# Moving work between stages in the second layer of a two-layer kernel: order of weight units, of the dt chain and of the turns

## The chip, the cores and the metric

The kernel runs on one core of one Trainium2 chip. The metric is the device time of one launch in microseconds (us): 1860.7 us is the median of three runs before the change (1860.04 to 1865.69).

Engines are named as the profile names them. PE is TensorE (matmuls and transposes; PEld its weight loads), DVE is VectorE, ACT is ScalarE, POOL is GpSimd, SP only issues the transfers of weights. Each engine runs its own list of instructions in order and waits on semaphores that the others raise.

## The reference, cut to what matters

The first block (an mLSTM and a sparse attention, then a mixture of 32 experts) is untouched by the change and is left out. The second block computes, for 256 tokens and a model width of 1024:

```python
h = rms_norm(x, norm_g) * (1 + scale) + shift
proj = h @ w_in
q, k, v, z_att, q_idx, k_idx, w_idx, z_ssm, xbc, dt_raw, gate_logits = split(proj)
q = partial_rope(rms_norm(q), ...); k = partial_rope(rms_norm(k), ...)
q_idx, k_idx = partial_rope(...), partial_rope(layer_norm(k_idx), ...)
o_att = sparse_attention(q, k, v, q_idx, k_idx, w_idx) * silu(z_att)      # top 64 causal keys
y_att = o_att @ w_branch_att
xs, bm, cm = split(silu(causal_conv(xbc) + conv_b))                         # 4 taps
dt = softplus(dt_raw + dt_bias); a = -exp(a_log)
y = ssd(xs, dt, a, bm, cm) + d_skip * xs                                    # chunks of 128
y = group_rms_norm(y * silu(z_ssm)) * ssm_norm_g
y_ssm = y @ w_branch_ssm
merged = sigmoid(g_att) * y_att + sigmoid(g_ssm) * y_ssm
x = x + gate * (merged @ w_out)
```

## The kernel before, in words

**Units of weights.** All of the second layer's weights pass through a list of 56 units (`UNITS2`) of 1 MB: 256 columns of a matrix with 1024 rows (or 128 columns of the one with 2048 rows). Units 0 to 7 give q, k, v, the indexer's parts and dt (unit 7 is only 100 columns wide); 8 to 11 (`U_ZA`) give z_att, the gate of the attention; 12 to 23 (`U_XBC`) feed the convolution; 24 to 39 (`U_ZS`) give z_ssm and the merging gates; 40 to 43 (`U_ATT`) are w_branch_att, 44 to 51 (`U_SSM`) w_branch_ssm, 52 to 55 (`U_OUT`) w_out. SP loads a unit into one of three raw slots (`load_unit`, L289) as soon as the unit three places earlier is done with its slot.

**Plain and split units.** A plain unit is multiplied in full fp32 straight from its slot, and the slot comes free when PE has used it. A split unit is first cut by ACT into a rounded high part (`make_high`, L1655) and by DVE into the rest (`make_low`, L1662), into one of three stages, and is multiplied in three cheaper passes (high with high, high with low, low with high); its slot comes free with the low part. Before, units 0, 1 and 12 to 23 are plain. `unit_by_tokens` (L1686) and `unit_by_columns` (L1698) are the two forms of the matmuls.

**Four programs, one after another.** The second layer is four `nc.Block()`s; at the end of each, every engine waits for all others.

1. Projections: PE runs units 0 to 7, DVE copies the results out of PSUM (L1770, L1773).
2. Attention (from L1822). PE calls `give(n)` for the next n of the 16 "halves", units 8 to 23, into the PSUM banks 0 and 1 in turn; ACT calls `take(n)` for them. A half of z_att is taken with one Silu into `azT` (L1861). A half of the convolution is taken with eight scaled copies (L1872, three of four into `taps`); POOL adds the taps (L1835) and ACT applies the Silu two halves later (`silu`, L1849). PE may give half h only when half h-2 is taken. Between the halves stand the steps of the attention: DVE normalises and rotates the index parts (L2004 to L2024), PE turns them (L1961, L1962), ACT and DVE form the norms of q and k (Square L1881, sums L2029, root L1885), DVE scales and rotates q and k (L2037 to L2040 and L1811 to L1816, twice), PE turns them (L1970), then logits (L1938), scores (L1946), the selection of keys on DVE (L2051 to L2072), exponentials on ACT (L1899), the turns of the probabilities (L1953, each copied by ACT, L1905) and the product with v (L1995, L1996).
3. State space (from L2127). PE turns xbc nine times (L2196) and ACT copies each (L2156, L2159); DVE works out dt and `adt` in 22 small steps (L2262 to L2279), PE sums them (L2201), DVE scales xs by dt (`y`, L2286). Then come eight pairs (chunk, group): `prepare(i)` on PE (L2213, L2216), masks and products on DVE (L2306, L2315), the exponential on ACT (L2165), the outputs (L2252), and between them two units each, called fills (units 24 to 39). Fills 16 to 19 are units 40 to 43 with the gated attention as the other factor, in its parts `inh` and `inl`.
4. Branch and output (from L2370). PE turns y (L2384), ACT and DVE form its parts yh and yl (L2417, L2441), PE multiplies by w_branch_ssm (L2394) and w_out, DVE adds the residual (L2461), PE turns the result, and it is stored.

The order in which the units stand in PE's program is written by hand; nothing plans it. Two lines set what is plain and what PE does between the turns of the probabilities:

```python
PLAIN = {0, 1} | set(range(U_XBC, U_ZS))
turn(1, 0); pe.wait_ge(sm("b_pt_ready"), 2); turn(1, 1); give(2)   # in short
```

Of the kernel before, what the change touches and what calls it, by code (L numbers as in the profile page):

```python
# [23 lines left out]
P = 128  # L24
# [129 lines left out]
UNITS2 += [("w_in_2", 0, [(0, P_QI, 256)]), ("w_in_2", 0, [(0, P_QI + 256, 68), (68, P_DT, 32)])]  # L154
U_ZA = len(UNITS2)
UNITS2 += halves("w_in_2", 0, P_ZA) + halves("w_in_2", 0, P_ZA + 512)
U_XBC = len(UNITS2)
UNITS2 += sum((halves("w_in_2", 0, P_XBC + 512 * n) for n in range(6)), [])
U_ZS = len(UNITS2)
# [9 lines left out]
PLAIN = {0, 1} | set(range(U_XBC, U_ZS))  # L169
# [32 lines left out]
def two_layers(nc, A, cst_in, c32_in, out):  # L202
    with ExitStack() as ctx:
# [1501 lines left out]
        bc = sb("bc", [P, 2 * HD + 2 * ID + 3 * SH])  # L1705
        att2 = ctx.enter_context(ExitStack())
# [71 lines left out]
        with ExitStack() as pi:  # L1778
# [12 lines left out]
            tmp = sb("tmp", [P, SEQ], at=pi)  # L1791
# [9 lines left out]

            HALVES = U_ZS - U_ZA
            ZHALVES = U_XBC - U_ZA
# [18 lines left out]
            with nc.Block() as block:  # L1822
# [6 lines left out]
                def _(pool):  # L1829
                    G.done(pool, pool.memset(taps[:], 0.0), sm("taps_zero"))  # L1830
                    for i in range(HALVES - ZHALVES):
                        pool.wait_ge(sm("half_taken"), ZHALVES + i + 1)
# [9 lines left out]
                def _(act):  # L1842
# [9 lines left out]
                    def take(count):  # L1852

                        for _ in range(count):
                            h = taken[0]
                            if h >= 2 and U_ZA + h + 2 in SPLIT:
                                make_high(act, U_ZA + h + 2)
                            act.wait_ge(sm("u_used"), U_ZA + h + 1)
                            src = ps[:, h % 2, :].rearrange("p (j t) -> p j t", j=2)
                            if h < ZHALVES:  # L1860
                                S.done(act, act.activation(azT[:, 2 * h:2 * h + 2, :], src, ACT.Silu), sm("half_taken"))  # L1861
                            else:
                                i = h - ZHALVES
# [13 lines left out]
                    make_high(act, U_ZA + 2)  # L1877
                    act.wait_ge(sm("var_ready"), 1)
                    S.done(act, act.activation(var[:], var[:], ACT.Sqrt), sm("dev_ready"))
                    for t in range(TT):  # L1880
                        S.done(act, act.activation(sq2[:], qkv[:, t, 0:NH * HD], ACT.Square), sm("head_sq"))  # L1881
                        if t == 0:
                            make_high(act, U_ZA + 3)
                        act.wait_ge(sm("head_sums"), t + 1)
                    S.done(act, act.activation(ssum[:], ssum[:], ACT.Sqrt), sm("head_rms"))  # L1885
# [4 lines left out]
                    take(3)  # L1890
# [27 lines left out]
                    for i in range(HALVES - ZHALVES - 2, HALVES - ZHALVES):  # L1918
                        silu(i)
# [176 lines left out]
        with ExitStack() as pj:  # L2096
# [31 lines left out]
            with nc.Block() as block:  # L2128
# [59 lines left out]
                def _(pe):  # L2188
# [66 lines left out]
                    for f in range(16, 20):  # L2255
                        fill(f)
# [246 lines left out]
```

## Time and profile before the change

| What | Value |
|---|---|
| median of three runs | 1860.7 us |
| the profiled execution | 1861.18 us |
| its span, first to last instruction | 1859.4 us |
| second layer in that span | from about 1379 us to the end |
| PE busy | 1740.1 us, 94% of the span |
| DVE busy | 555.9 us, 30% |
| ACT busy | 415.5 us, 22% |
| POOL busy | 106.4 us, 6% |
| mean granted clock of PE, in parts of full speed | 0.972 |

Times of rows are us from the start of the span. The profiled execution lies 0.5 us above the median, and 1.8 us of it lie outside its span. A matmul's end is modelled, so the pace of PE is read from starts: two groups of eight matmuls that start 0.96 us apart cost 0.12 us a matmul, whatever duration stands beside each. One fp32 matmul is two records.

### The profile page before, as it was taken

How to read it: one execution, taken by the hardware profiler on the slowest of the kernel's cores; microseconds unless marked ns; L12 is line 12 of the kernel's file. 1: busy time of each engine (PE TensorE's matmuls, PEld its weight loads, DVE VectorE, ACT ScalarE, POOL GpSimd, SP SyncE). 2: the span in 40 equal slices, each digit the busy share in tenths (PEclk: the TensorE clock that was granted, in tenths of full speed). 3: DMA queues.
4: the chain of work that ended last, by engine and by line, in shares of the span. 5: the costliest groups of instructions: out<-in, count | busy, mean ns of one | idle time of the engine just before them, and what ended most of it. 6: DMA issues, size and time to landing. Idle time of an engine off the chain costs nothing. (4 is left out here: it accounts for less than half of the span.)

```text
span 1859.4 us, 39736 instructions
## 1 busy us (share of the span) xinstructions
PE 1740.1 (94%) x17331; PEld 1017.3 (55%) x17331; DVE 555.9 (30%) x770; ACT 415.5 (22%) x692; POOL 106.4 (6%) x121
## 2 busy tenths in 40 slices
PE   6999998999999999999999999999859798799888
PEld 4875652343434434343443434344449787698888
DVE  2273172121111112111111211111346551676754
ACT  2344152000000000000000000000034266355442
POOL 0111020000000000000000000000000044110000
PEclk9999989999999999999999999999979899899999
DMA  9987395999999999999999999999616243333452
GB/s 344 345 286 244 133 338 210 388 396 407 401 397 399 399 398 395 400 398 393 392 403 404 394 399 397 399 398 408 226 51 196 63 135 93 113 116 112 136 148 80
DMA packets 187878, 545.45 MB, mean 293 GB/s; under 512 B 16216, under 2 KB 90216, under 8 KB 154952
## 3 DMA queue, kind: packets, MB, share of 16 engines
q1 hardware_dynamic: 172432, 519.49, 74.0%
q10 hardware_dynamic: 10968, 15.40, 2.3%
q0 software_dynamic: 4416, 9.69, 1.6%
q8 instruction: 44, 0.72, 0.2%
q14 instruction: 18, 0.15, 0.0%
HBM read 526.06 MB, written 17.84 MB: 293 GB/s over the span
## 5 line engine op out<-in xcount | busy, mean ns | idle before, releaser
L1428 PE MATMUL ps<-ring_low,xg 128*32 128x512 f32 x3072 | 344.6, 597 | 0.0
L1428 PE MATMUL ps<-first_ring,xg 128*32 128x512 f32 x3072 | 335.4, 592 | 0.0
L1559 DVE TENSOR_SCALAR gl<-ps 128x768 f32<-128x768 f32 x32 | 30.6, 957 | 684.1 <-PE ps L1428 684.1
L1428 PEld LDWEIGHTS ps<-first_ring,xg 128*32 128x32 f32 x3072 | 99.5, 110 | 230.1 <-issue 230.1
L1428 PEld LDWEIGHTS ps<-ring_low,xg 128*32 128x32 f32 x3072 | 96.4, 110 | 206.6 <-issue 200.8
L1451 PE MATMUL ps<-first_ring,aT 128*32 128x256 f32 x3072 | 173.3, 382 | 2.3 <-ACT aT L1510 2.3
L1451 PE MATMUL ps<-raw_more,aT 128*32 128x256 f32 x3072 | 171.6, 379 | 0.0
L1451 PEld LDWEIGHTS ps<-first_ring,aT 128*32 128x32 f32 x3072 | 100.4, 111 | 82.5 <-issue 20.2
L1504 ACT ACTIVATE sg<-gl 128x768 f32<-128x768 f32 x32 | 27.0, 844 | 510.8 <-DVE gl L1559 510.8
L1451 PEld LDWEIGHTS ps<-raw_more,aT 128*32 128x32 f32 x3072 | 99.9, 110 | 65.9
L1662 DVE TENSOR_TENSOR low<-ring_low,high 128x2048 fp32r<-128x2048 f32 x42 | 98.7, 2350 | 121.5 <-ACT high L1655 121.0
L1509 ACT ACTIVATE aT<-ps 128x576 f32<-128x576 f32 x32 | 20.8, 650 | 445.5 <-PE ps L1439 435.7
L1655 ACT ACTIVATE high<-ring_low 128x2048 fp32r<-128x2048 f32 x42 | 80.4, 1915 | 65.8 <-PE ps L2394 20.5
L1570 DVE COPY ye<-ps 128x768 f32<-128x768 f32 x32 | 30.6, 957 | 212.1 <-PE ps L1451 212.1
L1698 PE MATMUL ps<-hT,ring_low 128*128 128x256 f32 x384 | 86.1, 386 | 0.0
L1698 PEld LDWEIGHTS ps<-hT,ring_low 128*128 128x128 f32 x384 | 74.5, 195 | 10.6 <-ACT xbc L1872 0.3
L1398 POOL DMA_INDIRECT got<-y_dram,dest x8 | 7.6, 952 | 1075.8 <-DMA y_dram<-ye 1074.6
L1698 PE MATMUL ps<-inh,high 128*128 128x256 f32 x320 | 49.0, 293 | 16.1 <-ACT azT L1861 7.8
L321 PE MATMUL ps<-hT,first_ring 128*128 128x256 f32 x256 | 58.7, 389 | 1.8 <-ACT hT L514 1.8
L321 PEld LDWEIGHTS ps<-hT,first_ring 128*128 128x128 f32 x256 | 49.2, 194 | 11.5 <-issue 4.7
L1698 PEld LDWEIGHTS ps<-inh,high 128*128 128x128 f32 x320 | 43.2, 198 | 17.1 <-ACT azT L1861 8.1
L1835 POOL TENSOR_TENSOR xbc<-xbc,taps 128x512 f32<-128x512 f32 x36 | 46.1, 1279 | 102.5 <-ACT xbc L1872 100.5
(487 smaller groups left out, 1879.6 us busy)
## 6 DMA issues: line engine op xcount, KB each, us to landing
first_ring<-in_w_up_dram SPq DMA_DIRECT2D x128, 1024.0 KB, 6.6
ring_low<-in_w_up_dram SPq DMA_DIRECT2D x128, 1024.0 KB, 6.3
raw_more<-in_w_down_dram SPq DMA_DIRECT2D x64, 1024.0 KB, 6.7
first_ring<-in_w_down_dram SPq DMA_DIRECT2D x64, 1024.0 KB, 6.7
ring_low<-in_w_in_dram SPq DMA_DIRECT2D x39, 1024.0 KB, 5.3
first_ring<-in_w_ada_dram SPq DMA_DIRECT2D x7, 2048.0 KB, 20.3
ring_low<-in_w_ada_dram SPq DMA_DIRECT2D x5, 2048.0 KB, 18.2
y_dram<-ye ACTq DMA_DIRECT2D x32, 288.0 KB, 5.7
```

Of the source, the lines that this page charges most:

```text
L321: mm = pe.matmul(ps[:, bank, (j % 2) * SEQ:(j % 2 + 1) * SEQ], slots[n % len(slots)][:, k, j * P:(j + 1) * P], src[:, k, :], start=(k == 0 ...
L1398: pool.indirect_dma_start(got[:, t, BUFFER[j], :], None, y_dram[0:TOTAL, :], bass.IndirectOffsetOnAxis(dest[:, t, j:j + 1], 0))\
L1428: mm = pe.matmul(ps[32 * q:32 * q + 32, u, :], xg[:, k, 32 * block_of:32 * block_of + 32], w[:, :, 256 * f:256 * f + 256], start=False, st ...
L1451: mm = pe.matmul(ps[32 * q:32 * q + 32, 5 + u, 0:256], aT[:, f, 32 * block_of:32 * block_of + 32], w[:, 256 * part:256 * part + 256], star ...
L1504: act.activation(sg[:], gl[:], ACT.Sigmoid, scale=ALPHA).then_inc(s(tag, "sig_ready"), 1)
L1509: act.activation(aT[:, 0:6, :], flat[:, :, 0:ROWS], ACT.Copy).then_inc(s(tag, "aT_ready"), 1)
L1559: dve.tensor_scalar(gl[:], ps[:, 0:3, 0:256], LIMIT, None, ALU.min).then_inc(s(tag, "glu_ready"), 1)
L1570: dve.tensor_copy(ye[:], ps[:, 5:8, 0:256]).then_inc(s(tag, "ye_copied"), 1)
L1655: act.activation(high[:, s_ % STAGES], raw2[u % RAWS], ACT.Copy).then_inc(sm("u_high"), 1)
L1662: dve.tensor_tensor(low[:, s_ % STAGES], raw2[u % RAWS], high[:, s_ % STAGES].bitcast(F32), ALU.subtract)\
L1698: mm = pe.matmul(ps[:, bank, j * SEQ:(j + 1) * SEQ], a[:, k, j * P:(j + 1) * P], x[:, k, :], start=(i == 0), stop=(i == len(todo) - 1))
L1835: ins = pool.tensor_tensor(c, c, taps[:, i % 2, tap], ALU.add)
```

## The change

Nothing is computed that was not computed before; what moves is this.

- Units: the second half of z_att (two units) goes behind the convolution's twelve, so the halves are now z_att 0 and 1 (h = 0, 1), convolution 0 to 11 (h = 2 to 13), z_att 2 and 3 (h = 14, 15). Unit 7 and the first two of w_branch_att become plain.
- Attention: ACT takes two halves ahead of the second Square; PE gives two halves, and then one, around the turn of q and k, and one half between the turns (1, 0) and (1, 1). POOL clears only the first three columns of `taps`. The dt chain runs on DVE behind the probabilities, with its two exponentials on ACT in front of `exps(0)`; it lies in `rt`, the rotation's buffer, and `tmp` in `kd`.
- State space: the product of the attention with its gate opens DVE's program of this block. The sums of adt come first on PE, the nine turns use three banks and are copied by ACT and DVE two to one, fill 0 stands ahead of `prepare(0)`, and xs is scaled by dt one pair at a time. Fills 16 and 17 are plain; `inl` is formed after the last pair.
- Branch and output: fills 18 and 19 move into this block, behind the fourth and the eighth turn of y. w_out's units work in two banks each, and the residual is added after every second unit.

The diff, cut to its core:

```diff
-UNITS2 += halves("w_in_2", 0, P_ZA) + halves("w_in_2", 0, P_ZA + 512)
+UNITS2 += halves("w_in_2", 0, P_ZA)
 U_XBC = len(UNITS2)
 UNITS2 += sum((halves("w_in_2", 0, P_XBC + 512 * n) for n in range(6)), [])
+UNITS2 += halves("w_in_2", 0, P_ZA + 512)
...
-PLAIN = {0, 1} | set(range(U_XBC, U_ZS))
+PLAIN = {0, 1, U_ZA - 1} | set(range(U_XBC, U_ZS - 2)) | {U_ATT, U_ATT + 1}
...
-            tmp = sb("tmp", [P, SEQ], at=pi)
+            tmp = kd[:].rearrange("p t d -> p (t d)")
...
-                    G.done(pool, pool.memset(taps[:], 0.0), sm("taps_zero"))
+                    G.done(pool, pool.memset(taps[:].rearrange("p a b c t -> p (a b c) t")[:, :, 0:3], 0.0), sm("taps_zero"))
...
-                    make_high(act, U_ZA + 2)
                     act.wait_ge(sm("var_ready"), 1)
                     S.done(act, act.activation(var[:], var[:], ACT.Sqrt), sm("dev_ready"))
-                    for t in range(TT):
-                        S.done(act, act.activation(sq2[:], qkv[:, t, 0:NH * HD], ACT.Square), sm("head_sq"))
-                        if t == 0:
-                            make_high(act, U_ZA + 3)
-                        act.wait_ge(sm("head_sums"), t + 1)
-                    S.done(act, act.activation(ssum[:], ssum[:], ACT.Sqrt), sm("head_rms"))
+                    S.done(act, act.activation(sq2[:], qkv[:, 0, 0:NH * HD], ACT.Square), sm("head_sq"))
                     take(2)
                     act.wait_ge(sm("i_turned"), 1)
...
-                    take(3)
+                    act.wait_ge(sm("head_sums"), 1)
+                    S.done(act, act.activation(sq2[:], qkv[:, 1, 0:NH * HD], ACT.Square), sm("head_sq"))
+                    act.wait_ge(sm("head_sums"), 2)
+                    S.done(act, act.activation(ssum[:], ssum[:], ACT.Sqrt), sm("head_rms"))
+                    take(2)
                     act.wait_ge(sm("q_turned"), 1)
...
-                    take(3)
+                    take(4)
+                    S.done(act, act.activation(aexp, bcv("a_log_2"), ACT.Exp), sm("a_exp"))
+                    act.wait_ge(sm("dt_abs"), 1)
+                    S.done(act, act.activation(u_, u_, ACT.Exp), sm("dt_exp"))
                     exps(0)
...
                     mm.then_inc(sm("i_turned"), 1)
-                    give(3)
+                    give(2)
                     pe.wait_ge(sm("i_ready"), 1)
                     pe.wait_ge(sm("q_rotated"), TT)
...
                     mm.then_inc(sm("q_turned"), 1)
+                    give(1)
                     pe.wait_ge(sm("q_ready"), 1)
...
                     turn(1, 0)
+                    give(1)
                     pe.wait_ge(sm("b_pt_ready"), 2)
                     turn(1, 1)
-                    give(2)
+                    give(1)
...
-                    make_low(dve, U_ZA + 2)
...
-                    make_low(dve, U_ZA + 3)
...
+                    dve.wait_ge(sm("dt_exp"), 1)
+                    V.link(dve, dve.tensor_scalar(z_, u_, 2.0, None, ALU.add))
...
-                    for u in range(U_ZS, U_ZS + 2):
+                    for u in range(U_ZS - 2, U_ZS + 2):
                         make_low(dve, u)
-                    dve.wait_ge(sm("b_att"), 1)
-                    dve.wait_ge(sm("half_taken"), ZHALVES)
-                    V.link(dve, dve.tensor_tensor(azT ...
...
+            TURNS = [(0, 2), (1, 2), (0, 4), (0, 0), (1, 0), (0, 1), (1, 1), (0, 3), (1, 3)]
+            TURNED_IN = (0, 6, 7)
...
-                    pool.wait_ge(sm("adt_ready"), 1)
-                    pool.wait_ge(sm("xs_ready"), 9)
+                    pool.wait_ge(sm("xs_turned"), 2)
...
-                    pe.wait_ge(sm("xs_ready"), 9)
+                    pe.wait_ge(sm("az_gated"), 1)
+                    fill(0)
+                    pe.wait_ge(sm("xs_ready"), 6)
+                    pe.wait_ge(sm("xs_copied"), 3)
+                    pe.wait_ge(sm("cum_copied"), 1)
                     prepare(0)
...
-                    for f in range(16, 20):
+                    for f in range(16, 18):
                         fill(f)
...
+                    V.done(dve, dve.tensor_tensor(azT ..., ps[:, 2:6, :] ..., ALU.mult), sm("az_gated"))
...
-                    for t in range(TT):
-                        ins = dve.tensor_tensor(yv, xs[:, t, :] ..., dts[:, t, :] ..., ALU.mult)
...
                     for i, (c, g) in enumerate(PAIRS):
+                        V.link(dve, dve.tensor_tensor(heads(y[:, c, gw]), heads(xs[:, c, gw]),
+                                                      dts[:, c, gh].unsqueeze(2).to_broadcast([P, GH, SP]), ALU.mult))
...
-                    make_low(dve, U_ATT + 2)
+                    dve.wait_ge(sm("in_high"), 2)
+                    V.done(dve, dve.tensor_tensor(inl[:], azT[:], inh[:].bitcast(F32), ALU.subtract), sm("in_low"))
...
+                    for u in range(U_ATT + 2, U_SSM):
+                        make_low(dve, u)
...
+                    turn(range(4))
+                    unit_by_columns(pe, U_ATT + 2, 4, None, (inh, inl))
+                    turn(range(4, 8))
+                    unit_by_columns(pe, U_ATT + 3, 5, None, (inh, inl))
                     pe.wait_ge(sm("yh_ready"), 16)
...
-                        dve.wait_ge(sm("u_used"), U_OUT + k // 2 + 1)
+                        dve.wait_ge(sm("u_used"), U_OUT + 2 * (k // 4) + 2)
```

## Rows read from the trace of the kernel before

**Rows 1.** The page, busy time of an engine, its share and its instructions.
```profile
PE 1740.1 (94%) x17331; PEld 1017.3 (55%) x17331; DVE 555.9 (30%) x770; ACT 415.5 (22%) x692; POOL 106.4 (6%) x121
```

**Rows 2.** PE's waits from 1380 us on: us in total, times, longest.
```profile
PE ps L1698 <- ACT azT L1861: 7.8, 1, 7.8
PE ps L2213 <- DVE y L2286: 6.7, 1, 6.7
PE ps L1953 <- ACT qT L1905: 4.6, 1, 4.6
PE ps L2196 <- PEq L1822: 4.4, 1, 4.4
PE ps L2394 <- issue: 3.5, 1, 3.5
PE ps L1938 <- ACT kT L1894: 3.5, 1, 3.5
...
PE ps L1698 <- issue: 3.4, 1, 3.4
PE ps L2252 <- DVE xbc L2315: 2.7, 2, 2.5
PE ps L2213 <- DVE xbc L2306: 2.2, 6, 0.5
```

**Rows 3.** Timeline of PE: start, us, instructions, idle before them.
```profile
1424.54 1.00 PE L1686 MATMUL ps<-high,inh 128*128 128x100 f32 x8
...
1431.63 1.23 PE L1698 MATMUL ps<-inh,high 128*128 128x256 f32 x8 [1.63 <-PEq L1715]
...
1438.94 1.12 PE L1698 MATMUL ps<-inh,high 128*128 128x256 f32 x8
...
1444.70 0.38 PE L1961 MATMUL ps<-cst,idt 128*128 128x128 f32 x2
...
1466.36 7.07 PE L1698 MATMUL ps<-hT,ring_low 128*128 128x256 f32 x32
...
1610.30 1.95 PE L2216 MATMUL ps<-cst,xbc 128*128 128x128 f32 x16
```

**Rows 4.** A stretch in windows: engines' busy us, then granted clock, DMA share, GB/s.
```profile
1430.00:1436.10 6.10, 4.47 (x26) 4.50 (x26) 5.17 (x12) 3.20 (x2) 2.66 (x1) 0.72 0.56 169
```

**Rows 5.** Timeline of DVE and of ACT in the attention's first 50 us.
```profile
1451.51 0.28 DVE L2034 RECIPROCAL ssum<-ssum 128x20 f32<-128x20 f32 x1 [0.41 <-ACT ssum L1885]
...
1462.26 0.32 DVE L1816 TENSOR_TENSOR qkv<-rt 128x160 f32<-128x160 f32 x1
...
1473.52 1.20 ACT L1872 ACTIVATE taps<-ps,cols 128x253 f32<-128x253 f32 x3 [6.30 <-PE ps L1698]
```

**Rows 6.** Timeline of DVE and of POOL where both work in SBUF.
```profile
1508.83 1.37 DVE L2059 TENSOR_TENSOR sc<-sc,cst 128x256 f32<-128x256 f32 x1
...
1518.77 0.42 DVE L2065 TENSOR_TENSOR sc<-sc,cst 128x256 f32<-128x256 f32 x1
...
1508.38 1.54 POOL L1835 TENSOR_TENSOR xbc<-xbc,taps 128x512 f32<-128x512 f32 x1 [2.96 <-ACT xbc L1872]
```

**Rows 7.** Timeline of DVE: a step of dt, one of the loop, the residual.
```profile
1586.00 0.20 DVE L2265 TENSOR_SCALAR z_<-u_ 128x64 f32<-128x64 f32 x1 [1.40 <-ACT u_ L2150]
...
1655.60 0.69 DVE L2330 TENSOR_TENSOR t<-xs,bc 128x512 f32<-128x512 f32 x1
...
1853.14 1.00 DVE L2461 SCALAR_TENSOR_TENSOR xT<-ps,mod,xT 128x256 f32<-128x256 f32 x2 [4.75 <-PE ps L1698]
```

**Rows 8.** Timeline of ACT where y is turned.
```profile
1771.11 8.07 ACT L2417 ACTIVATE yh<-ps,cols 128x256 fp32r<-128x256 f32 x16 [5.72 <-PE ps L2384]
```

**Rows 9.** The page, transfers: issuer, count, KB each, median us to landing.
```profile
ring_low<-in_w_in_dram SPq DMA_DIRECT2D x39, 1024.0 KB, 5.3
```

**Rows 10.** Timeline of DVE: a low part that meets POOL, and one that does not.
```profile
1612.68 3.88 DVE L1662 TENSOR_TENSOR low<-ring_low,high 128x2048 fp32r<-128x2048 f32 x1
...
1631.00 2.29 DVE L1662 TENSOR_TENSOR low<-ring_low,high 128x2048 fp32r<-128x2048 f32 x1 [4.48 <-ACT high L1655]
```

## What the change will do to the time

> **What bounds the kernel now.** I read the page first. PE is busy for 94% of the span [rows 1], so its idle time is nearly all that a new order can win. Then PE's waits in the second layer [rows 2]: one long stall per stage. The six largest rows are 7.8, 6.7, 4.6, 4.4, 3.5 and 3.5 us, then come 3.4 and 2.7. Then PE's timeline [rows 3], for what a unit costs: the split unit from 1438.94 to 1444.70 costs 5.76 us, a plain one 32 records of 7.07 us, less a tail 6.9 us, and the 100 wide unit 7 takes from 1424.54 to the 1.63 us of idle before 1431.63, 5.5 us. A stall costs more than itself. The unit that starts at 1431.63 takes until 1438.94, 7.3 us against 5.76, and the window around it shows a granted clock of 0.72 of full [rows 4]: after the pause PE works for a while at the lower of its two levels (1.2 instead of 2.4 GHz). I price that at 1.5 us a stall [rows 3], up to 2.5 where turns follow.
>
> **The start of the attention.** Unit 7 plain: no row shows 100 columns in fp32. The nearest are fp32 records of 128 columns, 16 of them in 1.7 us by starts (the row says 1.95 with its tail) [rows 3], so 32 cost 3.4 us; by the plain unit's price it would be 6.9 at most, by columns alone 2.7. At 3.4 PE is done 2.0 us sooner, but the block ends with DVE's copy of idt, which stands behind the low part of unit 9. I take 0.9 us: **+0.9**.
>
> The 7.8 us before azT go. ACT was stuck between the two Squares and could not take the first half; now it takes it when PE has made it, at about 1439.9, and PE gives convolution 0 and 1 right behind the turn of the index parts (from about 1444.6 to 1458.4, two times 6.9). With the cold clock that is +9.3. The 3.5 us before the logits go too, covered by the third half, with their cold clock +4.9.
>
> But something is late next: q and k. Before, the scaling and rotation ran from 1451.51 to 1462.58 [rows 5], 11.1 us, and ended long before PE came. Now PE comes at 1458.4. ACT's second Square waits for the index turn (1444.6), the sums and the root come behind it, so DVE starts at about 1450.5, and alone would end at 1461.5. It is not alone. **DVE and POOL block each other**: an addition of 256 elements takes 0.42 us when POOL rests, and 1.37 us when it was asked at 1508.83, 0.45 us into an addition of POOL's, which ended at 1509.92 [rows 6]; it simply ran behind it. POOL's took 1.54 there. So where DVE works from SBUF to SBUF without a pause, each of POOL's additions (about 1.27 us) comes on top. ACT's copies of a half take about 3 us (three of eight in 1.20 [rows 5]), so convolution 0 reaches POOL at 1454.6 and convolution 1 at 1461.5: three additions each, 6 x 1.27 = 7.6 us, both inside DVE's stretch. q is ready at about 1469, and PE stands from 1458.4 for 10.4 us and then 2.0 more by the clock: -12.4. The bounds are 2.8 us of wait (no blocking, then 1.2 of clock) and 12 us (a table load of ACT more). I take the blocking because the rotation is of the same kind as the row's addition, two operands in SBUF. Together **+1.8**.
>
> The GPSIMD Engine Reference of the Trainium skill (section Specifications) says that GpSimd shares these with VectorE and contends with DVE instructions that have two SBUF inputs or a two-port mode. It speaks against this change, since it covers the rotation's small steps, which no row shows next to POOL; without it the wait would be 2.8 us. The row in [rows 6] agrees for an addition.
>
> **The rest of the attention.** The 4.6 us before turn (1, 1) are filled by a split unit of 5.76 us; with the cold stretch behind them (turns and the next unit, 2.5): **+7.0**. Its parts have to be there: the transfer can start when convolution 9 is used and lands 5.3 us later [rows 9], ACT and DVE need 4.2 more, and PE comes 15 us later. The block ended with ACT waiting for POOL's last addition and two Silus, 4.4 us of PE [rows 2]; now two units of z_att lie behind the convolution, and only the change of block stays, about 0.6: **+3.8**. dt's 22 steps of 0.20 us and more [rows 7] move into DVE's pause behind the probabilities. They too can meet six additions of POOL; that cover is about 10 us wide, and if it is gone, units 22 to 25 are late.
>
> **The start of the state space.** PE stood 6.7 us for `y` and, before that, ran nine turns at ACT's pace in the cold. From the block's start to fill 0 were 19.3 us, 3.8 of them `prepare(0)`. Now nothing waits for dt: the sums (0.8) and nine turns (4.7) with a short wait for DVE's copies, then fill 0, at about 6.7 us. Of the 15.5 before, 8.8 are saved, and 1.5 by the clock in `prepare(0)`; 0.7 to 0.8 come back, since no fill stands any longer between `prepare(0)` and `prepare(1)`, which waits for DVE's mask: **+9.5**.
>
> **The loop.** PE waits 6 times for DVE's mask, up to 0.5 us [rows 2]: the loop's circle runs through DVE and ACT, and PE follows. The change puts one more product into that circle in each pair, by the row of the same shape 0.69 us with 0.03 between [rows 7], six times in front of a `prepare`: **-4.4**. At its end the 2.5 us before the last outputs go, since units 40 and 41 are plain and ACT and DVE have no parts to make: **+2.5**.
>
> **Units 40 to 43 and the turn of y.** Before, from the last output to the first unit of w_branch_ssm, 41.2 us: 3.4 wait and 1.7 clock, four units 23.0, 2.4 between, and 10.1 for the turns, at ACT's pace of 1.0 us each [rows 8], 3.5 of it a plain wait. Now two plain units (13.8, 2.3 dearer than split) run beside DVE's last norm. Unit 43 can be fetched only when 40 is used, lands 5.3 us later [rows 9], is cut by ACT and DVE (4.2), and two products follow: the block ends 18.6 us behind the last output, PE having stood for 4.8. Then turns 2.1, a unit 5.8, turns 2.1, a unit 5.8, and 2.0 by the clock: 36.4. ACT and DVE are done with yh and yl before that. **+4.7**.
>
> **The end.** w_branch_ssm starts warm (1.6) and the second wait inside w_out's first unit goes (0.8): **+2.4**. But four residuals of 0.5 us [rows 7] follow the last matmul instead of two: **-1.0**.
>
> **The sum**: 0.9 + 1.8 + 7.0 + 3.8 + 9.5 - 4.4 + 2.5 + 4.7 + 2.4 - 1.0 = 27.2 us. From the profiled execution's 1861.2 that is 1834.0; it lies 0.5 above the median, so 1833.5 us, 1.5% less.
>
> **The rivals.**
> - POOL does not hold up the rotation: the wait for q is 2.8 us. For it: most of DVE's steps in the trace run alone, and the small ones may slip in between. Against: [rows 6]. It gives 8.4 more, 1825.
> - A collision inside the loop: the low part takes 3.88 us where it meets POOL and 2.29 where it does not [rows 10], and it begins only just behind POOL's work. If the new product shifts them onto each other in seven pairs, 7 x 1.6 = 11 us: 1845. Against: both start from the same event, so they should shift together.
> - The gaps only move: every stall returns behind the next step, and the time is 1860. Against: PE's work is the same and the new waits that I find have other work in front.
> - Slower: DVE as a whole becomes the bound in the attention. POOL's 36 additions of 1.27 us are 46 us; if DVE waits for all of them, 38 more than in my sum, at the rotation, the key selection and dt's chain, PE stands for each and the time is 1872. It decides once more than 27 us of them fall on a path that PE waits for; most fall on steps with slack, and before one met DVE for 1 us.
>
> **Chances.** The forecast's own mechanism 0.50, no blocking 0.25, the loop's collision 0.13, gaps that only move 0.04, slower 0.03; 0.05 for others, on the faster side. A run of this kernel can tell 0.3%, 5.6 us, from no change. So faster 0.93, same 0.04, slower 0.03. The range reaches from 1821 (no blocking, and the clock's costs halved) to 1846 (the collision).
>
> **What would show it.** In PE's waits: no azT, kT or qT row; a new row of L1970 behind DVE's rotation, some 10 us long, with DVE's L1811 to L2040 stretched while POOL adds; L2286 gone; `prepare` behind L2306 with about 1.2 us each; a gap of some 5 us before the turn of y. If the rotation's steps keep their 0.32 and 1.49 us while POOL works, the blocking step is wrong. If PE's wait for L2306 stays at half a microsecond, the loop is not bound by DVE. The forecast is wrong if the total of PE's waits falls by less than 15 us.

## The result and the profile after the change

The changed kernel takes **1830.25 us** (median of four runs, 1829.04 to 1831.8). Beside it the kernel before took 1863.14 us (four runs, 1860.04 to 1865.69). The ratio is 0.982, with a 95% interval from 0.9808 to 0.9833. A second series of the changed kernel (e11) gave 1830.61 (1829.72 to 1831.48), ratio 0.983 (0.9813 to 0.9846). The forecast was 1833.5, 27.2 us less than before; by the medians it is 32.9 us less. Part of that difference is the starting point: the median before the change that the forecast started from, 1860.7, lies 2.4 us below the one of all four runs.

The profiled execution took 1831.8 us with a span of 1830.0 and a mean granted clock of 0.978. The page's busy times, which answer to [rows 1]:

```profile
PE 1727.2 (94%) x17283; PEld 1004.4 (55%) x17283; DVE 562.6 (31%) x777; ACT 410.7 (22%) x688; POOL 106.8 (6%) x121
```

PE's waits from 1380 us on, against [rows 2] (us in total, times, longest):

```profile
PE ps L1688 <- PEq L220: 9.7, 1, 9.7
PE ps L1980 <- DVE qkv L1823: 9.3, 1, 9.3
PE ps L2386 <- PEq L2155: 6.5, 1, 6.5
PE ps L2230 <- DVE xbc L2310: 5.3, 7, 1.1
PE ps L2258 <- DVE xd L2301: 2.8, 3, 0.9
PE ps L2417 <- DVE inl L2489: 1.6, 1, 1.6
PE ps L1700 <- PEq L1719: 1.6, 1, 1.6
PE ps L2220 <- DVE bt L2289: 1.3, 1, 1.3
PE ps L2209 <- PEq L1829: 0.3, 1, 0.3
```

The first row is the entry into the second layer. It is ahead of that layer's first unit in both kernels, and is not counted below. The rest is 28.7 us, against 48.1 in the same view of before: 19.4 less. azT, kT, qT and `y` are gone. Three waits carry what is left: L1980 (the turn of q, behind the rotation), L2386 (the turn of y, behind the end of a block) and the loop's two rows, L2230 and L2258. PE's busy time fell as well, by 12.9 us, though its work is nearly the same. 11.3 us of it fell in the second layer, where the granted clock is 0.97 on average instead of 0.95: fewer stalls are followed by the slow clock.

By starts of PE's instructions, the stages add up as follows (before, after, gain in us). They sum to the 29.4 us between the two spans. That is less than the 32.9 us between the medians, since the profiled execution of the kernel before is a short one of its kind (1861.18 us) and that of the changed kernel the longest of its four.

| Stage | before | after | gain | forecast |
|---|---|---|---|---|
| everything ahead of the second layer | 1378.95 | 1380.10 | -1.15 | 0 |
| units 0 to 6 | 45.59 | 45.33 | +0.26 | 0 |
| unit 7 and the change of block | 7.09 | 5.34 | +1.75 | +0.9 |
| unit 8 to the turn of the index parts | 13.07 | 11.58 | +1.49 | 0 |
| from there to the end of the attention | 139.42 | 124.87 | +14.55 | +12.6 |
| start of the state space to the first outputs | 34.58 | 24.99 | +9.59 | +9.5 |
| the loop, first to eighth outputs | 118.84 | 120.32 | -1.48 | -1.9 |
| eighth outputs to the first unit of w_branch_ssm | 43.00 | 39.92 | +3.08 | +4.7 |
| w_branch_ssm and w_out | 72.33 | 69.95 | +2.38 | +2.4 |
| last turns and the end | 6.53 | 7.60 | -1.07 | -1.0 |
| sum | | | +29.4 | +27.2 |

The first line is work that the change does not touch. It moves from profile to profile: the second layer starts between 1377.16 and 1384.10 us in the profiles of this study. So two experiments are compared by their second layers too, from the first unit's start to the start of the last turns: 473.92 us before, 442.30 after.

### The profile page after: what moved, and what is told of

The parts are those of the page before. It is cut to its first block and busy times, and to the rows that moved or that the text cites. A ratio compares the mean times of both kernels' runs of the same rounds, so it can differ in the third digit from the quotient of the medians.

```text
span 1830.0 us, 39634 instructions
## 1 busy us (share of the span) xinstructions
PE 1727.2 (94%) x17283; PEld 1004.4 (55%) x17283; DVE 562.6 (31%) x777; ACT 410.7 (22%) x688; POOL 106.8 (6%) x121
## 5 line engine op out<-in xcount | busy, mean ns | idle before, releaser
L1664 DVE TENSOR_TENSOR low<-ring_low,high 128x2048 fp32r<-128x2048 f32 x39 | 91.4, 2346 | 73.4 <-ACT high L1657 73.0
L1657 ACT ACTIVATE high<-ring_low 128x2048 fp32r<-128x2048 f32 x39 | 74.7, 1916 | 43.1 <-PE ps L2404 17.3
L348 POOL DMA_DIRECT2D mrows<-mrow x56 | 28.1, 509 | 187.7 <-ACT mrow L341 187.7
L1424 PE MATMUL ps<-bup,one 96*32 96x512 bf16 x384 | 27.3, 386 | 8.2 <-ACT xg L1502 8.2
```

The source lines that it names most:

```text
L348: eng.dma_start(mrows[at:at + 4, :], mrow[32 * q:32 * q + 1, i % 2, :].rearrange("a (j p) -> a j p", p=P))\
L1424: pe.matmul(ps[32 * q:32 * q + 32, u, :], one3[:], cols_of, start=True, stop=False)
L1657: act.activation(high[:, s_ % STAGES], raw2[u % RAWS], ACT.Copy).then_inc(sm("u_high"), 1)
L1664: dve.tensor_tensor(low[:, s_ % STAGES], raw2[u % RAWS], high[:, s_ % STAGES].bitcast(F32), ALU.subtract)\
```

## The experiments

Diffs are against the changed kernel unless they say otherwise. "The layer" is the second layer's length as just defined.

**1. POOL held back until q and k are rotated** (e1). POOL's first sum of taps waits for the rotation; its three sums of the convolution's first half are then late, but nothing needs them yet.

```diff
                         pool.wait_ge(sm("half_taken"), XBC0 + i + 1)
+                        if i == 0:
+                            pool.wait_ge(sm("q_rotated"), TT)
```

> The changed kernel, but POOL's first convolution additions wait until q and k are rotated. Theory (POOL's six additions of 1.27 us block DVE's steps): the rotation's steps keep 0.33, 0.42, 1.2 and 1.5 us, DVE's stretch from its first step (L2044) to the last shrinks from 17.0 to 11.1 us by 6 us or a little less, PE's wait for q falls from 9.3 to about 3.3 us, with a little less of the slow clock behind it, and the time from 1830.3 to about 1823.5 us. Rival (the wait is long because DVE starts late, behind ACT's second Square and the root): the wait stays at 8 to 9 us and the time within 1.5 us of 1830.

Measured: 1823.05 us (1822.36 to 1824.5), ratio to the kernel before 0.9786 (0.9768 to 0.9804), and 7.6 below the changed kernel's second series. The layer is 435.76. First the changed kernel's DVE and then its POOL, by their timelines (start, us, instructions, idle before):

```profile
1452.98 0.33 DVE L1819 TENSOR_TENSOR rt<-qkv,sin 128x160 f32<-128x160 f32 x1
1453.34 1.44 DVE L1820 TENSOR_TENSOR rt<-qkv,cos 128x160 f32<-128x160 f32 x1
1454.82 1.31 DVE L1821 TENSOR_TENSOR rt<-qkv,sin 128x160 f32<-128x160 f32 x1
1456.16 1.31 DVE L1822 TENSOR_TENSOR qkv<-rt 128x160 f32<-128x160 f32 x1
...
1460.65 1.37 DVE L2050 TENSOR_TENSOR qkv<-qkv,bc 128x256 f32<-128x256 f32 x1
1462.05 1.27 DVE L1818 TENSOR_TENSOR rt<-qkv,cos 128x160 f32<-128x160 f32 x1
1463.36 1.30 DVE L1819 TENSOR_TENSOR rt<-qkv,sin 128x160 f32<-128x160 f32 x1
1464.69 0.33 DVE L1820 TENSOR_TENSOR rt<-qkv,cos 128x160 f32<-128x160 f32 x1
...
1453.34 3.96 POOL L1842 TENSOR_TENSOR xbc<-xbc,taps 128x512 f32<-128x512 f32 x3 [22.63 <-ACT xbc L1882]
1460.25 4.23 POOL L1842 TENSOR_TENSOR xbc<-xbc,taps 128x512 f32<-128x512 f32 x3 [2.96 <-ACT xbc L1882]
```

The same engines in e1, and its wait:

```profile
1450.91 0.33 DVE L1820 TENSOR_TENSOR rt<-qkv,cos 128x160 f32<-128x160 f32 x1
...
1457.89 8.00 POOL L1844 TENSOR_TENSOR xbc<-xbc,taps 128x512 f32<-128x512 f32 x6 [29.63 <-DVE qkv L1823]
1474.28 3.96 POOL L1844 TENSOR_TENSOR xbc<-xbc,taps 128x512 f32<-128x512 f32 x3 [8.38 <-ACT xbc L1884]
...
PE ps L1982 <- DVE qkv L1823: 3.3, 1, 3.3
```

Six DVE steps, one for each addition of POOL's, take 1.27 to 1.44 us instead of 0.33 or 0.42. That adds 5.9 us; in e1 all keep their length, and the wait falls from 9.3 to 3.3. The expectation's rival, that DVE starts late, falls: DVE's first step comes 69.0 us after the layer's start in both.

**2. The loop's product moved into its slack** (e2, e10). In e2 the scaling of xs for pair i+1 stands behind `seg_ready` of pair i. In e10 both chunks are scaled at once, ahead of the loop.

```diff
-V.link(dve, dve.tensor_tensor(y of pair i, xs, dts, ALU.mult))   # in front of the mask of pair i
+if i == 0: scale(0)
...
                                                       ALU.min), sm("seg_ready"))
+if i + 1 < len(PAIRS): scale(i + 1)
```

> The changed kernel, but the scaling of xs by dt for the next pair stands right behind the mask of this pair, where DVE waits for ACT, instead of in front of the next mask. Theory (the loop's circle runs through DVE and ACT, and the product lengthens it by 0.72 us a pair): PE's waits for L2310 and L2301 fall from 8.1 us together to about 3 to 4, and the time by 4 to 5 us, to about 1825.8. Rival (PE bounds the loop, the waits are only its reading): no change beyond 1 us.

> The changed kernel, but xs is scaled by dt at once in front of the loop, two products of 2.3 us as before the change, with fill 0 where the change put it. Theory (the product lengthens the loop's circle, and at the start of the stage DVE has slack behind fill 0: it is idle from 1577.5 to 1581.8 but for that one product): 4.4 us less than the changed kernel, as with the scaling in the slack, and nothing lost in front: about 1825.8. Rival (the bulk products come back onto the path in front of the first mask): 2 us or more are lost again, 1828 and above.

Measured: e2 1825.47 us (1824.99 to 1825.9), ratio 0.9798 (0.978 to 0.9815), layer 437.47; e10 1824.72 (1823.58 to 1825.46), ratio 0.9798 (0.9781 to 0.9814). The loop of e2 takes 115.95 us instead of 120.32. PE's waits in e2, against 5.3 and 2.8 above, and the same to the digit in e10:

```profile
PE ps L2230 <- DVE xbc L2317: 3.1, 7, 0.8
PE ps L2258 <- DVE xd L2308: 0.6, 3, 0.2
```

The waits give 4.4 us and the loop 4.4. So the product was on the circle that PE follows: where it stood it cost most of its 0.72 us a pair, and where e2 or e10 put it, about nothing.

**3. The block's end** (e3, e12). In e3 the two gated products of units 40 and 41, the low part of unit 43, and SP's load of unit 46 move into the next block; e12 moves SP's load alone.

```diff
-                    for u in range(U_ZS + 2, U_SSM + 3):      # SP in the state space's block
+                    for u in range(U_ZS + 2, U_SSM + 2):
...
-                    for u in range(U_SSM + 3, len(UNITS2)):   # SP in the last block
+                    for u in range(U_SSM + 2, len(UNITS2)):
```

> The changed kernel, but unit 43's low part and the two gatings of fills 16 and 17 stand at the start of DVE's next program instead of at the end of this one. Theory one (as read in the trace of after: DVE works without a pause from the last output to the end of the block, so DVE sets its end): PE's wait of 6.5 us in front of the turn of y falls by about 3.5 us, the slow stretch behind it by up to 1 us, the time to about 1826 us. Theory two (as forecast: the transfer of unit 43, which waits for the plain unit 40, and its high part set the end): the block ends only when ACT has the high part of unit 43, 1728.4 in the trace of after, and the wait falls too but ends there: a difference of at most 3.7 us, and the last instruction before the block's end is ACT's. Rival: the work pushed behind the turns delays yl and w_branch_ssm by what was gained: 1830.

> The changed kernel with SP's load of unit 46 moved behind the boundary of the last block, and nothing else; the low part of unit 43 and the two gated products stay ahead of it. In the changed kernel DVE was through at 1732.11, but the next block's first turn started at 1734.76, and SP's load of unit 46, which waits for that low part, takes 1730.82 to 1734.31. Theory: the last of the three ends the block, so with SP's load gone the block ends with DVE, the turns start 0.5 to 1.2 us behind its last product (0.53 in the row of the kernel before), from the seventh output to the first turn it is 20.3 to 20.9 us instead of 22.2, and the time falls by 1.5 to 2, to about 1828.7. Rival 1: DVE alone held the block and the 2.6 us behind it are the change of blocks itself; then the stretch stays at 22.2 and the time at 1830.4. Rival 2: the load is late at the other end, unit 46 comes too late for PE and a wait of over 1 us appears in the units of w_branch_ssm, so that the time stays or rises.

Measured: e3 1823.21 us (1822.9 to 1826.79), ratio 0.9791 (0.9771 to 0.9811), layer 436.45; e12 1828.7 (1826.7 to 1830.78, five runs), ratio 0.982 (0.9806 to 0.9833). The changed kernel's DVE, SP and PE around the boundary (timeline):

```profile
1726.30 4.49 DVE L1664 TENSOR_TENSOR low<-ring_low,high 128x2048 fp32r<-128x2048 f32 x2
1730.71 1.40 DVE L2354 TENSOR_TENSOR ring_low<-ring_low,ps 128x512 f32<-128x512 f32 x2
...
1730.82 3.49 SPq L291 DMA_DIRECT2D ring_low<-in_w_branch_ssm_dram  x1
...
1734.76 3.65 PE L2386 MATMUL ps<-cst,y 128*128 128x128 f32 x16 [6.47 <-PEq L2155]
```

e12's:

```profile
1728.39 4.50 DVE L1664 TENSOR_TENSOR low<-ring_low,high 128x2048 fp32r<-128x2048 f32 x2
1732.81 1.40 DVE L2354 TENSOR_TENSOR ring_low<-ring_low,ps 128x512 f32<-128x512 f32 x2
...
1734.76 3.36 PE L2386 MATMUL ps<-cst,y 128*128 128x128 f32 x16 [4.37 <-PEq L2155]
```

and e3's SP and PE:

```profile
1725.94 1.78 SPq L291 DMA_DIRECT2D ring_low<-in_w_branch_ssm_dram  x1
...
1728.17 1.94 PE L2379 MATMUL ps<-cst,y 128*128 128x128 f32 x16 [2.67 <-PEq L2155]
```

In the changed kernel DVE is done at 1732.11 and SP's issue at 1734.31; the turns start 0.45 us behind SP. In e3 it is 0.45 behind SP again (1725.94 + 1.78 = 1727.72), DVE having ended at 1725.79. In e12 DVE is done at 1734.21 and the turns start 0.55 behind it. So the last of them ends the block, and SP counts.

What makes SP late is not DVE's low part alone. The issue of unit 46 starts 0.03 us behind that low part, and then lasts 3.49 us. It is the third load in 2.5 us: unit 44's was issued at 1728.32, when PE was done with unit 41, and unit 45's at 1728.73. Unit 44 landed 6.1 us after its issue, at 1734.44, by this row of the transfers (the last figure is the time from issue to landing):

```profile
ring_low<-in_w_branch_ssm_dram SPq DMA_DIRECT2D x1, 1024.0 KB, 6.1
```

The issue of unit 46 ended at 1734.31, 0.13 us before that. In all eight profiles that have these three loads (the changed kernel's, e1, e2, e4, e6, e10, e11 and e12) that issue ended within 0.16 us of unit 44's landing, also in e12, where it started at 1734.71 and lasted 1.75 us. So in the changed kernel the block's end follows the landing of unit 44; whether a faster DVE alone would have brought it forward was not tried, and these rows speak against it. What the issue waits for is not shown beyond this coincidence.

From the eighth outputs to the turns it is 22.23 us, 20.14 in e12 and 18.44 in e3. The late load of e12 costs nothing: its waits have no row for it. Its layer is 437.28 us, 5.0 shorter than the changed kernel's, but only 3.1 of that lie around the boundary; 1.3 come from units 0 to 6 and 0.6 from the attention, which the edit does not touch. Its median is 1.9 below the second series of the changed kernel (e11), with ranges that overlap, so the conclusion rests on the rows.

**4. Fill 0 back behind the first `prepare`** (e4).

```diff
-                    fill(0)
                     pe.wait_ge(sm("xs_ready"), 6)
...
-                        if i:
-                            fill(2 * i)
+                        fill(2 * i)
```

> The changed kernel, but fill 0 stands behind the first prepare again. Theory (the 9.6 us of this stage come from dt's chain and the bulk scaling having left the path, not from fill 0's place): PE waits 1 to 2 us more for the copies in front of prepare, and the 0.85 us wait for the first mask goes: 0 to +1.5 us, 1830.3 to 1831.8. Rival (fill 0 covers the stage's waits): +4 us or more, 1834 and above.

Measured: 1831.93 us (1831.52 to 1832.54), ratio 0.9831 (0.9814 to 0.9849). From the state space's start to the first outputs 25.07 us, against 24.99. Its median is 1.3 us above the second series of the changed kernel, but the second layer is as long (442.53 us against 442.30). What the place of fill 0 wins in front it loses as the wait of `prepare(1)`. So the 9.6 us owe nothing to it. By the waits 6.7 of them are dt's chain (the row of `y` in [rows 2]); how the rest divides between the turns' copies and the clock was not tried apart.

**5. Single parts put into the kernel before** (e5, e8). e5 gives one half between turn (1, 0) and turn (1, 1), e8 makes unit 7 plain; diffs against the kernel before.

```diff
                     turn(1, 0)
+                    give(1)
                     pe.wait_ge(sm("b_pt_ready"), 2)
                     turn(1, 1)
-                    give(2)
+                    give(1)
```

```diff
-PLAIN = {0, 1} | set(range(U_XBC, U_ZS))
+PLAIN = {0, 1, U_ZA - 1} | set(range(U_XBC, U_ZS))
```

> The kernel before, with one line of the change alone: the last half but one is given between turn (1, 0) and turn (1, 1). Theory (a stall costs itself and the slow clock behind it, 4.6 + 2.5 us): the wait of L1953 goes and the time falls by 7.0 us. Rival (the gap moves to the end of the block, where ACT and POOL finish the last half): the wait at the block's end, 4.4 us, grows by what was gained, and the time stays within 1.5 us.

> The kernel before, with unit 7 plain alone. Theory (read from the trace of after: unit 7 costs PE 1.75 us less, and the stretch behind it is not at the slow clock, 1.5 us, but the wait for azT is set by ACT and DVE, which start only 1.75 us sooner): unit 8 takes 5.8 us instead of 7.3, the wait for azT grows from 7.8 to about 9.3, and the time falls by 1.8 us. As forecast (DVE's low part of unit 9 holds the block's end): 0.9 us. Rival: all of it stays, 3.3 us.

Measured: e5 1859.24 us (twelve runs, 1857.62 to 1862.27), ratio 0.9977 (0.9968 to 0.9986), so 0.23% or 4.3 us gained. By the stages the turns' part is 7.4 shorter, and the next two are 1.9 and 1.3 longer. PE's wait at the end of that block in e5, against 4.4 in [rows 2]:

```profile
PE ps L2197 <- PEq L1822: 6.3, 1, 6.3
```

The 1.9 us come back there, since ACT and POOL end the block at their own pace (in e5 POOL adds six times without a pause, from 1569.96 to 1579.89, and ACT's last Silu ends at 1580.89), and PE only arrives sooner. With the z_att units behind the convolution this wait is 0.3 us, so there the half between the turns keeps its price. These stages add up to 4.2 us, as the medians have it. The profiled execution's whole layer, though, is as long as before (473.84 us against 473.92): the other 4.1 us went in stages that the edit does not touch, ahead of the turns of the probabilities and in w_branch_ssm. e8 took 1861.79 (twelve runs, 1859.81 to 1865.61), ratio 0.999 (0.9981 to 0.9999). It starts unit 8 1.75 us sooner, as the changed kernel does, and unit 8 runs 1.5 faster; by the start of the first plain unit all but 0.6 is given back: the wait for azT is 8.4 instead of 7.8, and the turn of the index parts waits 1.6 us for DVE. (Its profiled execution is its longest, 1865.61 us, so its layer, 476.77, says nothing of the gain.) DVE was held by POOL's clearing of `taps`, by e8's timeline:

```profile
1431.45 2.23 DVE L2006 TENSOR_SCALAR idt<-idt,mean 128x64 f32<-128x64 f32 x1
...
1430.97 2.66 POOL L1830 MEMSET taps<- 128x3072 f32 x1 [78.64 <-POOLq L1715]
```

The same step takes 0.26 us a moment later. In the kernel before it was held for the same 2.23 us, but PE came later. The change clears three columns only (0.13 us of POOL), an edit that I had named and not costed, and takes two low parts of 2.29 us out of the same stretch of DVE. The 2.0 us of the clearing alone cover the 1.6; the two edits were not tried apart.

**6. The third half ahead of q's turn** (e6).

```diff
-                    give(2)      # behind the turn of the index parts
+                    give(3)
...
-                    give(1)      # behind q's turn
```

> The changed kernel, but PE gives the third half in front of the turn of q and k instead of behind it. Theory (DVE sets when q is ready, at 1466.2, whatever PE does): the wait for q falls by 6.9 us to 2.4, but ACT's copies of q and k, 3.5 us, are uncovered behind it; together 3.4 us less wait and up to 1 us less at the slow clock: 1826 to 1827. Rival (a third half keeps ACT and POOL busy earlier and holds DVE up again): no gain, 1830.

Measured: 1827.08 us (1825.99 to 1829.2), ratio 0.9811 (0.9795 to 0.9828), 3.5 less than the changed kernel's second series. PE's waits in e6:

```profile
PE ps L1948 <- ACT kT L1902: 3.0, 1, 3.0
...
PE ps L1980 <- DVE qkv L1823: 2.4, 1, 2.4
```

The 9.3 us become 2.4, and kT's wait comes back, 3.0 us where [rows 2] had 3.5. A unit can cover one of the two; holding POOL back (e1) is worth twice as much.

**7. All three together, and the tail** (e7, e9). e7 is e1, e2 and e3 in one. e9 also gives w_out's last two units one bank each, so that only two residuals follow the last matmul.

> The changed kernel with the three edits together that each took some us: POOL's first additions behind the rotation, the scaling in DVE's slack, unit 43's low part behind the block's end. If they act in different stages they add up: 1830.3 - 7.2 - 4.8 - 7.0 = 1811.3 us. If one only exposes another's wait, 1815 or more.

> The same three, and w_out's last two units in one bank each as before the change, so that two residuals instead of four follow the last matmul: 1.0 us less than with the three alone, about 1810.3 us. If the tail is set by something else (the copies, the store), no change against it.

> The changed kernel once more, unchanged, as the mark for the two runs beside it, because the first layer, which no edit touches, has begun the second up to 3 us sooner or later from kernel to kernel: 1829 to 1832 us, with the second layer's stages as in the first profile within 1.5 us together.

Measured: e7 1816.12 us (1814.89 to 1816.56), ratio 0.9742 (0.9723 to 0.976), layer 426.89; **e9 1815.15** (1813.17 to 1815.7), ratio 0.9736 (0.9717 to 0.9755), layer 426.73, which beats both kernels, the changed one by 15 us. The three parts shorten the layer by 6.5, 4.8 and 5.9 us alone, 17.2 in all, and by 15.4 together. PE's waits in e7:

```profile
PE ps L1982 <- DVE qkv L1823: 3.3, 1, 3.3
PE ps L2232 <- DVE xbc L2319: 3.1, 7, 0.8
PE ps L2390 <- PEq L2157: 2.8, 1, 2.8
```

They are those of the single runs. What is missing is clock. The turns of y and the two units among them take 16.68 us in e7 and 15.03 in e3, which is 1.65 of the 1.8 us, though PE stood for 2.8 and 2.7 us ahead of them. The four us around the first turns in windows, e3 and then e7 (busy time of PE, PEld, DVE, ACT and POOL, then granted clock, DMA share, GB/s):

```profile
1728.00:1732.00 4.00, 3.83 (x34) 3.86 (x35) 3.76 (x4) 2.97 (x7) 0.00 (x0) 1.00 1.16 308
```

```profile
1720.60:1724.60 4.00, 4.00 (x23) 4.00 (x23) 3.90 (x5) 2.91 (x7) 0.00 (x0) 0.60 1.18 303
```

e11 is the changed kernel again, as above. e9's tail is not told from e7 by the medians, whose ranges overlap. The profiles show it: from the last turns to the end it is 6.55 us in e9 and 7.58 in e7 (7.56 to 7.68 in all ten profiles with the change's w_out), the 1.0 us that was expected.

## Why the prediction was right, and where its steps were off

The direction, the mechanism of each large term and the size were right: 27.2 us forecast for the profiled execution, 29.4 measured. That the sum came so near is in part luck. Three stages gave 4.3 us more than forecast (unit 7, unit 8, the rest of the attention), the units 40 to 43 gave 1.6 less, and the first layer, which nobody touched, took 1.15 back in this profile.

**The start of the attention.** The price of unit 7 held: 3.71 us, where the forecast had 3.4 and the kernel before 5.46 (7.09 less the 1.63 of idle). PE's timeline:

```profile
1425.43 3.71 PE L1688 MATMUL ps<-ring_low,hT 128*128 128x100 f32 x32
1430.77 1.19 PE L1700 MATMUL ps<-inh,high 128*128 128x256 f32 x8 [1.63 <-PEq L1719]
```

I had taken only 0.9 of the 2.0 us, since DVE's copy stands behind the low part of unit 9. But unit 7 takes no stage any longer, so unit 9's parts wait for unit 5 and not for unit 6. They are done early, DVE's copy waits for PE alone (4.94 us idle ahead of it), and 1.75 came, the whole price of unit 7. And unit 8 now runs at the full clock (below), 1.5 us that I had not counted.

**q and k, and the blocking.** The step forecast a wait of 10.4 us, and 9.3 came, ending at 1466.2 where about 1469 was forecast. Experiment 1 shows the mechanism, and with it the first rival (1825, no blocking) falls. DVE began at 1449.1, 1.4 us earlier than I had it. And POOL cost 5.9 us, not 7.6: I had put 1.27 on top for each addition, but a stretched step is 1.31 in all, so it costs 1.31 - 0.33 = 0.98; DVE's own 0.33 lies beside an addition of POOL's, and the pace of the first three, 1.32 (3.96 in all), is the one that they have with DVE idle. The Trainium skill has this in SBUF — State Buffer (section Terms): the port pair that VectorE and GpSimd share is locked for a whole instruction, and the other engine blocks. The trace agrees for the 160 element steps, 0.33 us alone and about 1.3 next to POOL.

The fear for dt's chain came true as well: six of its steps met POOL. One of them in the changed kernel's DVE timeline, behind a step that did not:

```profile
1534.23 0.23 DVE L2099 TENSOR_TENSOR rt<-rt 128x64 f32<-128x64 f32 x1
1534.48 1.27 DVE L2100 TENSOR_SCALAR rt<-rt 128x64 f32<-128x64 f32 x1
```

No wait of PE's answers to them; the pause behind the probabilities held.

**The clock behind the stalls** was rightly counted. The changed kernel in windows (columns as in experiment 7): unit 8; PE's wait and then the turn of q; the wait before and the turn of y.

```profile
1430.00:1436.00 6.00, 5.24 (x44) 5.27 (x45) 4.64 (x23) 2.77 (x3) 0.13 (x1) 1.00 0.99 313
...
1457.00:1466.20 9.20, 0.00 (x0) 0.00 (x0) 8.82 (x12) 3.02 (x8) 4.37 (x4) 0.69 0.38 114
1466.20:1470.50 4.30, 4.26 (x20) 4.29 (x21) 0.38 (x2) 0.00 (x0) 0.00 (x0) 0.50 0.02 4
...
1728.00:1734.70 6.70, 0.29 (x2) 0.00 (x0) 4.07 (x4) 0.35 (x1) 0.00 (x0) 0.92 0.84 224
1734.70:1738.00 3.30, 3.24 (x16) 3.27 (x17) 0.99 (x3) 1.99 (x5) 0.00 (x0) 0.50 1.19 292
```

0.50 is the lower of the two levels, 1.2 GHz of 2.4. The 20 transposes of q and k take 4.3 us there and the first 16 of y 3.3, against 1.7 for 16 in the full clock (1.67 from start to start, 1744.94 to 1746.61). I had added 2.0 us in each place; it was 2.2 behind the wait for q, and at the turn of y 1.6 and 1.1 more in the unit behind it (6.88 against 5.76).

**The rest of the attention** gained 14.6 us with the above, against 12.6 forecast. The block's end gave 4.1 (3.8). The rest, 10.5, is the turns' part and the stage of q, forecast 8.8; how much falls to each depends on what is allowed for plain and split units that changed places between them. **The start of the state space** was 9.6 (9.5).

**The loop.** The step "the change puts one more product into that circle" was right in kind and in size: experiment 2 takes the product out of the circle and gains 4.4 us, the term of the sum. PE's single waits in the loop are 0.5 to 1.1 us, where about 1.2 each was forecast. The loss of the stage was 1.5 us, where 1.9 was forecast. The second rival (1845) needed the low parts to collide with POOL in seven pairs; in the changed kernel one low part is stretched, to 3.36 us in the first pair, as one was before, and all later ones take 2.29.

**Units 40 to 43 and the turn of y** is the term that was mis-sized most, 3.1 instead of 4.7, by its step "the block ends 18.6 us behind the last output, PE having stood for 4.8". PE stood for 6.5. The clock took 0.7 more than I had, and the turns without it 0.8 less (1.7 for 2.1, twice), so the wait is what was mis-sized. The step took the transfer of unit 43 as what is late. The rows of experiment 3 show otherwise: unit 43 landed at 1726.40 and its high part was done at 1728.35, before DVE was through with the low part of unit 42. DVE works without a pause into the boundary, and behind it SP's last load ends the block, 2.2 us later. I had counted the products but not SP, which every block waits for too, nor that the issue of its third load in a row would last until the first had landed. (The waits and stretches that I listed for this stage before the change add up to 40.6 us and not to 41.2; by starts it is 43.0 less the 1.7 of the outputs, 41.3.)

**The end** came as worked out. The total of PE's waits fell by 19.4 us, above the 15 below which I had called the forecast wrong. The third rival (gaps only move) and the slower one fall by the stage table: two places got a new wait of weight, q and y, and POOL's additions were paid for at one of them. The key selection, which the slower rival needed, keeps its step lengths beside POOL (below). What stays open is what holds unit 46's issue for 3.5 us, when one that stands alone takes 0.37; the runs show with what it ends, the landing of unit 44, not what it is made of.

## What to carry to other kernels

Before GpSimd's work is moved beside a chain of small VectorE steps, count one wait per GpSimd instruction (0.98 us each here, beside additions of 1.27); the same work held back behind the chain was free here. At a block boundary ask which engine ends last, the engine that only issues transfers included: here three loads were issued in 2.5 us just ahead of the boundary, and the third held all engines until the first had landed. And put a loop's extra product behind the signal that the bound engine waits for, not ahead of it.

## What the runs showed of the hardware

- A collision of POOL and DVE is paid for by the one that asks while the other works, and not every DVE step takes part. An addition of POOL takes 1.26 us with DVE idle, and at most 1.32 beside the short steps of the rotation, which grow to 1.3 us. But it took 1.49 us when it was asked during DVE's scaling of 1.22 us (1460.25), and 3.24 us behind a low part of 2.45 us (its row in the changed kernel; the low part runs from 1548.80 to 1551.25):

```profile
1549.17 3.24 POOL L1842 TENSOR_TENSOR xbc<-xbc,taps 128x512 f32<-128x512 f32 x1
```

  MAX8 and MATCH_REPLACE8 keep 0.29 and 0.28 us beside POOL. dt's TENSOR_SCALAR, with one tensor as its input, is stretched (0.20 to 1.27), and three additions take 3.96 us beside the key selection too. DVE in e1, while POOL added from 1474.28 to 1478.24:

```profile
1475.29 0.29 DVE L2076 MAX8 top<-sc 128x8 f32<-128x128 f32 x1
...
1475.70 0.28 DVE L2077 MATCH_REPLACE8 sc<-top,sc 128x128 f32<-128x128 f32 x1
```

- The clock after a short pause was not set by the pause alone. The same 1.63 us pause before unit 8 left a granted clock of 0.72 in the kernel before [rows 4], where split units of fewer columns ran ahead of it, and 1.00 in e8, which differs only in unit 7 being plain (32 full fp32 matmuls):

```profile
1430.00:1437.00 7.00, 5.84 (x49) 5.87 (x50) 5.14 (x14) 2.21 (x2) 2.66 (x1) 1.00 0.98 303
```

  In all eleven profiles of the changed kernel and its variants the pause is the same and unit 8 runs at its full pace, and in both without a plain unit 7 (the kernel before and e5) it is slowed. Behind the 2.7 and 2.8 us pauses of e3 and e7 the clock was 1.00 and 0.60 though PE did the same in both; that difference is not explained.
- SP's issue of a 1 MB load takes 0.37 us when it stands alone. Close behind one another the second and the third take more: 0.58 and 1.49 us behind the one at 1567.17, 1.82 and 3.49 us behind the one at 1728.32, in the changed kernel.
